# Expert chunks of a product-key expert layer, repacked by the step that uses them

## The reference

```python
def chunk(xc):
    q = (xc @ wq).reshape(c, PEER_HEADS, 2, half)
    sc = jnp.einsum('thid,ikd->thik', q, keys).astype(jnp.float32)
    top_s, top_i = lax.top_k(sc, PEER_TOPK)
    cand_s = top_s[:, :, 0, :, None] + top_s[:, :, 1, None, :]
    cand_i = top_i[:, :, 0, :, None] * PEER_NKEYS + top_i[:, :, 1, None, :]
    best_s, best_pos = lax.top_k(cand_s.reshape(c, PEER_HEADS, -1), PEER_TOPK)
    idx = jnp.take_along_axis(cand_i.reshape(c, PEER_HEADS, -1), best_pos, axis=-1)
    gate = jax.nn.softmax(best_s, axis=-1)
    ue = u[idx]
    ve = v[idx]
    act = jax.nn.gelu(jnp.einsum('td,thkd->thk', xc, ue).astype(jnp.float32), approximate=False)
    return jnp.einsum('thk,thkd->td', (gate * act).astype(xc.dtype), ve)
```

## Time and profile before

| | us |
|---|---|
| median of 3 runs | 2989.59 (2984.39 to 2993.38) |
| profiled execution | 2979.47 |
| its span | 2977.8 |
| TensorE busy | 2846.4 (96%) |
| VectorE busy | 1781.1 (60%) |
| TensorE's time at line 2516, busy | 683.1 |
| at line 2505, busy and idle before it | 298.3 and 44.5 |

### The profile page before, as it was taken

How to read it: one execution, slowest core, us unless ns; L and a number is a source line. 1 busy time by engine, 2 the same in 40 slices (tenths; PEclk the granted TensorE clock), 3 DMA queues, 4 the chain that set the end, 5 groups by cost and what they waited for, 6 DMA issues and landing times.

```text
span 2977.8 us, 46537 instructions
## 1 busy us (share of the span) xinstructions
PE 2846.4 (96%) x17164; PEld 2591.0 (87%) x17164; DVE 1781.1 (60%) x4030; ACT 920.1 (31%) x1939; POOL 330.5 (11%) x397
## 2 busy tenths in 40 slices
PE   8999999999998999999999899989999999999998
PEld 5888888779887888999998899978889999998998
DVE  6888888556666876879333333268678793333432
ACT  4222322334764664126111000046631351110000
POOL 0000000000000000029111111000000381111100
PEclk9999999999999999999999999999999999999999
DMA  7333333223223333783687788523447746877983
GB/s 292 115 123 114 123 114 114 85 80 138 86 86 114 111 131 129 264 314 129 239 296 287 279 334 330 207 99 114 143 133 294 266 143 255 299 295 274 346 318 116
DMA packets 101184, 575.32 MB, mean 193 GB/s; under 512 B 9072, under 2 KB 9456, under 8 KB 52144
## 3 DMA queue, kind: packets, MB, share of 16 engines
q1 hardware_dynamic: 79936, 420.23, 39.6%
q0 software_dynamic: 21104, 153.23, 13.4%
HBM read 572.38 MB, written 1.05 MB: 193 GB/s over the span
## 4 chain that ended last, share of the span: by engine, by line
PE 82%; DMA 7%; DVE 5%; issue 2%; ACT 2%; DVEq 1%; ACTq 0%; POOL 0%; SPq 0%; POOLq 0%
PE bank L2516 19%; PE bank L2457 11%; PE bank L494 10%; PE bank L496 9%; PE bank L495 9%; PE bank L2505 7%; DMA wring<-in_w_peer 7%; PE bank L2490 2%; PE bank L1676 2%; PE bank L2477 2%; PE bank L997 1%; PE bank L986 1%; PE bank L1370 1%; PE bank L1388 1%; DVE arena L2796 1%
## 5 line engine op out<-in xcount | busy, mean ns | idle before, releaser
L2516 PE MATMUL bank<-arena,wring 128*128 128x192 f32 x4096 | 683.1, 326 | 0.3 <-DMA wring<-in_w_peer 0.3
L2516 PEld LDWEIGHTS bank<-arena,wring 128*128 128x128 f32 x4096 | 668.7, 190 | 2.3 <-issue 2.3
L478 DVE TENSOR_TENSOR peer_r<-wring,peer_r 128x512 fp32r<-128x512 f32 x440 | 296.2, 697 | 215.2 <-ACT peer_r L473 212.2
L494 PE MATMUL bank<-h_r,peer_r 128*128 128x512 f32 (+1 forms) x1088 | 397.0, 365 | 5.4 <-DVE h_r L508 3.3
L496 PE MATMUL bank<-h_r,peer_r 128*128 128x512 f32 (+1 forms) x1088 | 384.2, 353 | 0.0
L2571 POOL DMA_INDIRECT arena<-in_experts,arena x128 | 154.6, 1208 | 1873.6 <-DVE arena L2773 1011.6
L2505 PE MATMUL bank<-res,wring 128*128 128x192 f32 x1664 | 298.3, 334 | 44.5 <-DMA wring<-in_w_peer 44.0
L473 ACT ACTIVATE peer_r<-wring 128x512 fp32r<-128x512 f32 x440 | 266.6, 628 | 231.3 <-PE bank L496 227.8
L495 PE MATMUL bank<-h_r,peer_r 128*128 128x512 f32 (+1 forms) x960 | 333.7, 348 | 0.0
L2505 PEld LDWEIGHTS bank<-res,wring 128*128 128x128 f32 x1664 | 273.7, 192 | 61.8 <-issue 37.8
L2457 PE MATMUL bank<-res,wring 128*128 128x192 f32 x1920 | 313.1, 326 | 0.0
(11 more groups left out here) (403 smaller groups left out, 4118.1 us busy)
## 6 DMA issues: line engine op xcount, KB each, us to landing
wring<-in_w_peer SPq DMA_DIRECT2D x256, 1024.0 KB, 5.6
wring<-in_w_proj SPq DMA_DIRECT2D x34, 1024.0 KB, 4.8
wring<-in_w_hy SPq DMA_DIRECT2D x32, 1024.0 KB, 5.1
arena<-in_w_ada POOLq DMA_DIRECT2D x16, 1024.0 KB, 5.1
wring<-in_w_out SPq DMA_DIRECT2D x16, 1024.0 KB, 4.8
wring<-in_w_ada SPq DMA_DIRECT2D x8, 1024.0 KB, 10.1
wring<-in_w_hyout SPq DMA_DIRECT2D x8, 1024.0 KB, 4.9
wring<-in_w_q SPq DMA_DIRECT2D x8, 1024.0 KB, 4.8
```

The lines of the kernel that those rows point to most:

```text
L478: v.tensor_tensor(SPLIT[:, buf, 1, :], raw_quarter(name, i, j, q), SPLIT[:, buf, 0, :].bitcast(F32), ALU.subtract).then_inc(split_lo, 1)
L494: pe.matmul(out_ap, w_hi, x_hi, start=start, stop=False, **kw)
L2516: mm = pe.matmul(expert_sum(k), wring[:, s, at + k * P:at + (k + 1) * P], GP[:, par, :], start=False, stop=True, skip_group_check=True)
```

## The change

Chunks of the main stage are packed anew: chunk 0 holds u of 0 and u of 1; chunk c+1 holds u of c+2 and v of c, which step c uses; the last one holds v of 50 and v of 51. There are 52 as before. Each v product in the main stage now waits for the landing of the chunk it reads. GpSimd frees chunk 0 when the second u product is done (`u_done`), chunk n+1 when v of n is done, and the last chunk after v of 51. In HBM all expert chunks of a layer lie in the order of use, each whole: 8 KB for each partition in one run, in pre, mid and post as well, and `stream_pairs` goes.

```diff
--- before.py
+++ after.py
@@ -438,17 +438,6 @@
         def stream(sp, name, src, n):
             for i, j in turns(sp, n):
                 stream_chunk(sp, name, src, i, j, i * RING + j)
-
-
-
-
-
-        def stream_pairs(sp, name, src, first, n):
-            for i, j in turns(sp, n):
-                s, r = slot_of(name, i, j)
-                sp.wait_ge(chunk_done[s], r + 1)
-                sp.dma_start(wring[:, s, :].rearrange("p (a c) -> p a c", a=2),
-                             src[first + RING * i + j]).then_inc(w_landed[s], 16)
 
         split_chunks = lambda name, n: {"proj": len(SPLIT_CHUNKS)}.get(name[:-1], n)
         SPLIT_PHASES = [(name, split_chunks(name, n)) for name, n, _ in PHASES
@@ -2497,51 +2486,49 @@
             for k in range(KT):
                 pe.matmul(expert_sum(k), ident, dense(k), start=(k % 2 == 0), stop=(k % 2 == 1))
 
-            def first_product(i, j):
-                w = wait_chunk(pe, f"peer{l}", i, j)
+            def first_product(i, j, chunk, at):
+                w = wait_chunk(pe, f"peer{l}", i, chunk)[:, at:at + D]
                 b, use = bank_of(f"peer{l}", i, j)
                 pe.wait_ge(bank_free[b], use + 1)
                 for k in range(KT):
                     mm = pe.matmul(bank[b][:, 0:TD], w[:, k * P:(k + 1) * P], dense(k), start=(k == 0), stop=(k == KT - 1))
                 mm.then_inc(u_done, 1)
 
-            def rows_product(n, par, place):
-
-                name, i, j, at = place
-                s, r = slot_of(name, i, j)
+            def rows_product(n, par, name, i, chunk, at):
+
+                w = wait_chunk(pe, name, i, chunk)[:, at:at + D]
                 pe.wait_ge(gp_ready, GP0 + BLOCKS * l + n + 3)
-                if name[:4] == "post":
-                    pe.wait_ge(w_landed[s], 16 * (r + 1))
                 for k in range(KT):
-                    mm = pe.matmul(expert_sum(k), wring[:, s, at + k * P:at + (k + 1) * P], GP[:, par, :],
-                                   start=False, stop=True, skip_group_check=True)
+                    mm = pe.matmul(expert_sum(k), w[:, k * P:(k + 1) * P], GP[:, par, :], start=False, stop=True,
+                                   skip_group_check=True)
                 mm.then_inc(v_used, 1)
 
-            main = lambda i, j: (f"peer{l}", i, j, D)
-            post = lambda i, q: (f"post{l}", i, q // 2, (q % 2) * D)
-            first_product(0, 0)
-            first_product(0, 1)
+            def main_step(i, j):
+                first_product(i, j + 2, j + 1, 0)
+                rows_product(RING * i + j, j % 2, f"peer{l}", i, j + 1, D)
+
+            first_product(0, 0, 0, 0)
+            first_product(0, 1, 0, D)
             with pe.Fori(0, MAIN // RING - 1) as i:
                 for j in range(RING):
-                    first_product(i, j + 2)
-                    rows_product(RING * i + j, j % 2, main(i, j))
+                    main_step(i, j)
             last = MAIN // RING - 1
-            for j in range(RING):
-                if j + 2 < RING:
-                    first_product(last, j + 2)
-                rows_product(RING * last + j, j % 2, main(last, j))
+            for j in range(RING - 2):
+                main_step(last, j)
+            for half in range(2):
+                rows_product(MAIN - 2 + half, half, f"peer{l}", last, RING - 1, half * D)
             full, rest = divmod(KEPT, 2 * RING)
             with pe.Fori(0, full) as i:
                 for q in range(2 * RING):
-                    rows_product(MAIN + 2 * RING * i + q, q % 2, post(i, q))
+                    rows_product(MAIN + 2 * RING * i + q, q % 2, f"post{l}", i, q // 2, (q % 2) * D)
             for q in range(rest - 1):
-                rows_product(MAIN + 2 * RING * full + q, q % 2, post(full, q))
+                rows_product(MAIN + 2 * RING * full + q, q % 2, f"post{l}", full, q // 2, (q % 2) * D)
             pe.wait_ge(gathered, GATHERED0 + l + 1)
             for half in range(2):
                 for part in range(2):
                     pe.matmul(mix_acc(0, half)[0:NG, :], ident[:, part * NG:(part + 1) * NG],
                               GACC[:, half * 512:(half + 1) * 512], start=(part == 0), stop=(part == 1))
-            rows_product(BLOCKS - 1, 1, post(full, rest - 1))
+            rows_product(BLOCKS - 1, 1, f"post{l}", full, (rest - 1) // 2, D)
 
         def gather_gate(act, l, g):
 
@@ -2682,9 +2669,11 @@
                 a.then_inc(hot_b, 1)
                 if n - 4 in TABLE_AT:
                     issue(TABLE_AT[n - 4] + GRING)
+            pool.wait_ge(u_done, U0 + MAIN * l + 2)
+            pool.sem_inc(chunk_done[slot_of(f"peer{l}", 0, 0)[0]], 1)
             for n in range(BLOCKS):
-                if n < MAIN or (n - MAIN) % 2:
-                    name, k = (f"peer{l}", n) if n < MAIN else (f"post{l}", (n - MAIN) // 2)
+                if n < MAIN - 2 or n % 2:
+                    name, k = (f"peer{l}", min(n + 1, MAIN - 1)) if n < MAIN else (f"post{l}", (n - MAIN) // 2)
                     pool.wait_ge(v_used, BLOCKS * l + n + 3)
                     pool.sem_inc(chunk_done[slot_of(name, *divmod(k, RING))[0]], 1)
                 if n - 1 in VALUES_AT:
@@ -2857,11 +2846,10 @@
                 stream(sp, f"proj{l}", A[f"w_proj{l}"], 17)
                 stream(sp, f"out{l}", A[f"w_out{l}"], 8)
                 stream(sp, f"wq{l}", A[f"w_wq{l}"], 4)
-                two = A[f"w_peer{l}"].rearrange("(n a) p c -> n p a c", a=2)
-                stream_pairs(sp, f"pre{l}", two[:, :, :, 0:KT * P], (MAIN + MID) // 2, EARLY // 2)
-                stream_pairs(sp, f"mid{l}", two[:, :, :, 0:KT * P], MAIN // 2, MID // 2)
-                stream(sp, f"peer{l}", A[f"w_peer{l}"], MAIN)
-                stream_pairs(sp, f"post{l}", two[:, :, :, KT * P:], MAIN // 2, KEPT // 2)
+                up, at = A[f"w_peer{l}"], 0
+                for name, n in (("pre", EARLY // 2), ("mid", MID // 2), ("peer", MAIN), ("post", KEPT // 2)):
+                    stream(sp, f"{name}{l}", up[at:at + n], n)
+                    at += n
             for k2 in range(4):
                 sp.wait_ge(end_act if k2 % 2 else end_dve, k2 // 2 + 1)
                 sp.dma_start(two_tiles(out, k2), two_tiles(h, k2)).then_inc(stored, 16)
@@ -3130,7 +3118,11 @@
         arrays[f"w_wq{l}"] = tiles(a["peer_wq_2"][l], range(8), KT)
         u = a["peer_u_2"][l].reshape(P, BLOCKS, KT, P).transpose(1, 3, 2, 0).reshape(BLOCKS, P, D)
         v = a["peer_v_2"][l].reshape(P, BLOCKS, D).transpose(1, 0, 2)
-        arrays[f"w_peer{l}"] = np.concatenate([u, v], 2)
+        u_of = [*range(MAIN + MID, BLOCKS), *range(MAIN, MAIN + MID)]
+        up = [(u[a], u[b]) for a, b in zip(u_of[0::2], u_of[1::2])]
+        up += [(u[0], u[1]), *((u[n + 2], v[n]) for n in range(MAIN - 2)), (v[MAIN - 2], v[MAIN - 1])]
+        up += [(v[n], v[n + 1]) for n in range(MAIN, BLOCKS, 2)]
+        arrays[f"w_peer{l}"] = np.stack([np.concatenate(pair, 1) for pair in up])
         arrays[f"experts{l}"] = np.concatenate([a["peer_u_2"][l], a["peer_v_2"][l]], 1)
     return {k: np.ascontiguousarray(v) for k, v in arrays.items()}
```

## The result

The changed kernel took 2917.31 us (median of four runs, 2914.89 to 2919.89) against 2991.49 us before, a ratio of 0.9747 with a 95% interval of 0.9711 to 0.9783. It is faster by 74 us where 65 were forecast. In the two profiled executions the spans are 2977.8 and 2913.8 us, 64.0 us apart.

What follows compares the result with a forecast made beforehand. TensorE, busy 96%, was held to be bound by late expert chunks in the main stages. 2979.5 less 65.2 us, all other terms 0, gave 2914.3 us profiled, carried over to a median of 2924 us; range 2908 to 2946 us.

Steps and rivals of the forecast that it cites:

- The pace and the excess: Main stages: 101 products at 2.60 us make 262.6 us per layer; the 65.2 us beyond that in two layers go.
- From the profiled execution to the median: Whole kernel: the timed median's 10.1 us above the profiled execution carries over, 2914.3 to 2924.4 us.
- rival D: Whole kernel: the 10.1 us between profiled and median run are chunk waits too and go, 2914 us; chance 0.12.
- The cause: Main loop's first product: a load had one step, 5.20 us, before its use; repacking gives three, 15.6 us, less hand-over.
- sign that loads would land later than 5.1 us: Main stage chunk loads: times to landing longer than 5.1 us, yet harmless.
- The clock: TensorE, main stages: slow groups behind waits vanish with the waits; if they stayed, the sum would lose about 5 us.
- Bandwidth: Main stages: 312 GB/s at a DMA share of 0.85, under what was delivered elsewhere; cost 0.
- the extra waits: Main loop v products: 104 more waits on chunk landings, always met; taken as 0, at most 11 us.
- the release of the first chunk: GpSimd, main stage: one added wait per layer before its first gather of the stage; cost 0.
- The gathers: Main stage: late next; VectorE waits some 4 us more often, but a margin of 5 us makes it cost nothing.
- Rival A: Pre stage: larger packets delay the routing's gathers, 11 us per layer, 22 in all, 2946 us; chance 0.03.
- Rivals B and E: Main stages: B, loads late in bursts, 2957 us, chance 0.05; E, slot releases still late, 2989 us, chance 0.02.

Runs made afterwards that it cites:

- lag2: The changed kernel with chunk c+1 freed two steps later; 2989.59 us, ratio 1.0005 to the kernel before.
- repack_only: The kernel before with only the main chunks repacked and released as in the changed kernel, pre, mid and post as before; 2912.91 us, ratio 0.9752.
- before_nogather: The kernel before without the 32 gathers of each main stage; 2926.10 us, ratio 0.9779.
- before_again: The kernel before, unchanged, one more profiled execution without comparison; span 2975.9 us.
- gather_late2: The changed kernel with each gather of main and post issued two blocks later; 2984.80 us, ratio 0.9985 to the kernel before.
- lag1_again: The changed kernel with chunks freed one step later, timed again beside the changed kernel on one chip; 2917.05 us, ratio 0.9741.
- repack_again: Repacking alone, with two runs of 4 KB in pre, mid and post, timed again beside the changed kernel; 2916.31 us, ratio 0.9735.
- after_again: The changed kernel, unchanged, timed and profiled again; 2915.04 us, ratio 0.9735 to the kernel before.
- gather_late1: The changed kernel with each gather of main and post issued one block later; 2928.00 us, ratio 0.9783 to the kernel before.
- lag1: The changed kernel with chunk c+1 freed one step later; 2910.75 us, ratio 0.9752 to the kernel before.
- layout_only: The kernel before with u and v of one block per chunk, but all chunks whole in order of use; 2993.93 us, ratio 1.0029.

## Why the prediction was right, point by point

- **The pace and the excess.** The pace is right to the digit: 262.60 us in both layers. The excess of 65.2 us is 0.3 too large, since it mixes the starts and ends of two views; by one view it is 64.9. The spans differ by 64.0 us, as outside the main stages the two executions differ by 0.9 us the other way. The sum had the profiled execution at 2914.3 us; it took 2915.43.
- **From the profiled execution to the median.** This step of the forecast was off. It carried over unchanged that the median lay 10.1 us above the profiled execution; in the changed kernel it lies 1.9 above. So 2917.31 us is nearer to rival D's 2914 than to the forecast's 2924.
- **The cause.** Shown: lag2 takes back the lead and the time comes back; repack_only gives it and the gain is there. That one step is what a load had before is confirmed from the other side by before_nogather: loads of 4.8 us are late by little. The prediction's sign that loads would land later than 5.1 us and do no harm can't be read: the changed kernel's trace gives no time to landing for its chunks.
- **What an idle us costs.** 44.0 us idle made an excess of 64.9. Three groups at the lower clock gave 4.8 us (4.54, 4.36 and 4.47 us for 2.86). Each of the 33 listed waits also costs 0.26 us that isn't listed, the overlap of 0.16 us with the group before and 0.10 us of a group that starts empty: 8.6 us. The other 7.5 us lie in 36 late starts too short to be listed, seen as groups of 2.81 to 2.87 us. Elsewhere it was alike: 38.0 us of waits went with an excess of 56.5 (lag2), 38.5 with 60.8 (before_again). In gather_late2, 46.7 us of waits went with 67 us of time.
- **The clock.** After waits of 2.10 and 2.17 us groups ran slow (and a third after 2.89 us), after 2.33 us one didn't, nor after 2.63 us in the second layer. The windows of the slow group at 1642.11 and of the one behind the 2.63 us show that it was the clock, granted at 0.61 in the one and 1.00 in the other:

```profile
2713.18 2.87 PE L2505 MATMUL bank<-res,wring 128*128 128x192 f32 x16 [2.63 <-DMA wring<-in_w_peer]
...
1642.11:1646.49 4.38, 4.38 (x17) 4.38 (x18) 0.89 (x1) 0.00 (x0) 0.32 (x1) 0.61 0.97 383
...
2713.18:2715.90 2.72, 2.72 (x17) 2.72 (x18) 0.00 (x0) 0.00 (x0) 0.00 (x0) 1.00 0.85 355
```

  The slow groups went with the waits, and both stages show 1.00. The Trainium skill, "TensorE: Matmul & The Clock Gate", section "Part 1: The HAM clock gate", says that the array falls to the lower rate when it has been idle. By the means of the stages the traces agree, 0.99 with the waits and 1.00 without; by single waits the length alone does not tell which one is followed by a slow group.
- **Bandwidth, the extra waits, the release of the first chunk.** Each costs nothing, as taken: 101 products at 2.60 us leave no room for 104 waits of any size, nor for a late release of chunk 0, whose slot the u product of block 5 reads next.
- **The gathers.** That VectorE would wait for them more often is not borne out by the changed kernel's first trace: 22.7 us in 10 places (row below), where before it was 19.9 in 10. Its second trace has 27.8 us in 11 and lag1_again 37.1 in 20, against 21.8 in 11 in before_again, so how much more it is stays open. Of 32 gathers in a main stage only 4 have four steps to the third next; the others have five. The margin of 5 us holds in the main stage alone. At the border to the post stage the step is half as long and a delay of one block already shows, 4.21 us.
- **Rival A** (packets and the routing): its price was nothing, but its mechanism leaves a trace. VectorE idles 13.9 us behind the routing in the changed kernel as in the earlier trace rows and has no wait for a gather in the pre stage, and repacking with and without the layout takes the same time. Beside each other in that stage, loads and gathers do depend on the layout. In the second layer the median load took 5.7 to 5.9 us in the traces with two runs of 4 KB (before, before_again, before_nogather, repack_again) and 4.9 to 5.2 with one run of 8 KB (after_again, lag1_again, gather_late1 and 2); in the first layer it was 5.0 to 5.8 against 4.9 to 5.3. The median gather took 8.3 to 9.7 us with the first and 8.8 to 10.6 with the second, both layers together: somewhat more, not the third that the rival wanted, and the 13.9 us cover it. That the size of the runs is what does this is read from few traces; no run tests it alone. Below, the two rows of the table of waits of the changed kernel (the second in the pre stage of layer 0), then the second layer's pre stage in before (2181 to 2351 us) and in lag1_again (2150.4 to 2320.4).

```profile
DVE arena L2546 <- DMA arena<-in_experts,arena: 22.7, 10, 3.3
...
DVE arena L2785 <- ACT arena L2611: 13.9, 1, 13.9
...
wring<-in_w_peer SPq DMA_DIRECT2D x30, 1024.0 KB, 5.8
arena<-in_experts,arena POOLq DMA_INDIRECT x13, 8.8
...
wring<-in_w_peer SPq DMA_DIRECT2D x30, 1024.0 KB, 4.9
arena<-in_experts,arena POOLq DMA_INDIRECT x13, 10.4
```

- **Rivals B and E** (loads late in bursts; releases late): fallen; no load is late, and even two steps are enough (lag1).
- **Rival D** (more is won in ordinary runs) had 0.12 and is partly borne out: ordinary runs gained 74 to 79 us, traces 64. Profiled executions of kernels with chunk waits lie under the median of their timed runs, by 10.1 (before), 11.8 (before_again), 12.0 (layout_only) and 17.9 us (lag2); those of kernels without such waits lie within 6 us of it (2915.43 and 2917.31 in the changed kernel). The timed runs of before spread over 18 to 34 us, by the set, those of the changed kernel over 5 and 7. That the loads wait longer in unprofiled runs fits all of this but is argued, not shown: no trace holds an unprofiled run.

## What to carry to other kernels

A ring of n slots gives a load n steps less those for which its data stays pinned. What counts is which halves of a buffer are used in the same step, not in the same item: pack together what is consumed together, and the lead grows without a byte of memory. Read the lead from the trace (release of a slot to the use of its successor), set the longest load beside it, not the median, and include what shares the DMA engines. When the lead is long enough, look for the next item at the borders of a stage too, where a step is shorter.

## What the runs showed that I had not expected

- The load of 1 MB took 4.8 us alone and 5.1 us in the median beside gathers, but up to 7.9 us; those few tenths in the median hide what some 54 of the 65 us came from, since with a lead of 4.75 us every lengthening counts.
- In the second layer's pre stage, loads in one run of 8 KB for each partition landed sooner than in two of 4 KB beside gathers, 4.9 to 5.2 us against 5.7 to 5.9, and the gathers beside them mostly later. This kernel's time shows neither, since nothing waits for them there.
- TensorE's listed waits understate what they cost by a third: 64.9 us for 44.0 listed.
- The timed runs of the kernels with late loads scatter over 18 to 35 us (before, layout_only, lag2), those of the changed kernel, repack_only and lag1 over 5 to 9. before_nogather, with the short lead but even loads, scatters over 6.4 us. That it is the varying length of the loads that a short lead passes on fits this, but no trace of several runs shows it.
